# Starting a decoder trunk sooner: half a first weight unit, x through a second DMA queue, the first norm summed on VectorE, and a third unit inside that norm

## The reference

```python
hn = rmsnorm(x, norm_mix_pre[0])                 # x * rsqrt(mean(x*x) + 1e-6) * gain
proj = einsum('bsd,de->bse', u, w_in)            # u = hn
z, xBC, dt = split(proj, ...)
xBC = silu(causal_dwconv(xBC, conv_w, conv_b))   # width 4
dt = softplus(dt + dt_bias)                      # 32 heads
A = -exp(A_log)
# ssd_chunked: cumulative sums of dt*A along each chunk of 128 tokens, their exponentials, ...
```

## Time and profile before

| | |
|---|---|
| time, median of 3 runs | 1522.05 us (1521.98 to 1523.62) |
| profiled execution | 1520.41 us, of which the span is 1518.4 us |
| TensorE busy | 1460.5 us, 96% of the span |
| VectorE busy | 1021.9 us, 67% |
| ScalarE busy | 613.2 us, 40% |
| GpSimd busy | 192.4 us, 13% |
| DMA | 142.10 MB, 94 GB/s mean |

### The profile page before, as it was taken

How to read it: one execution, slowest core, us unless ns; L and a number is a source line. 1 busy time by engine, 2 the same in 40 slices (tenths; PEclk the granted TensorE clock), 3 DMA queues, 4 the chain that set the end, 5 groups by cost and what they waited for, 6 DMA issues and landing times.

```text
span 1518.4 us, 20441 instructions
## 1 busy us (share of the span) xinstructions
PE 1460.5 (96%) x6774; PEld 1162.1 (77%) x6774; DVE 1021.9 (67%) x1428; ACT 613.2 (40%) x953; POOL 192.4 (13%) x123
## 2 busy tenths in 40 slices
PE   6999999999998999999999999999789999999996
PEld 5778888888786788888888767776568888888885
DVE  6888898889427787778422667778357877776223
ACT  5654555557324323322322436565443332233221
POOL 3011100111113000000011332222121000000111
PEclk9999999999999999999999999999889999999998
DMA  4433323332221222223322121111121322223221
GB/s 150 156 125 124 138 98 137 124 138 70 84 90 63 98 97 86 94 97 105 103 95 86 54 70 56 69 55 55 42 97 56 97 97 97 95 87 112 95 95 55
DMA packets 36277, 142.10 MB, mean 94 GB/s; under 512 B 4048, under 2 KB 4176, under 8 KB 34192
## 3 DMA queue, kind: packets, MB, share of 16 engines
q1 hardware_dynamic: 36240, 141.62, 27.1%
HBM read 139.38 MB, written 2.23 MB: 93 GB/s over the span
## 4 chain that ended last, share of the span: by engine, by line
PE 75%; issue 10%; DVE 7%; POOL 3%; ACT 3%; DMA 1%; DVEq 0%; SPq 0%; POOLq 0%; ACTq 0%
PE bank L395 17%; PE bank L396 16%; PE bank L397 16%; PE b_x L395 6%; PE b_x L397 6%; PE b_x L396 6%; POOL w_lo L350 3%; DVE w_lo L358 1%; DVE cv_s L812 1%; PE b_y L828 1%; ACT w_hi L344 1%; PE b_y L395 1%; PE b_y L396 1%; PE b_y L397 1%; PE b_x L840 1%
## 5 line engine op out<-in xcount | busy, mean ns | idle before, releaser
L358 DVE TENSOR_TENSOR w_lo<-raw,w_hi 128x1024 fp32r<-128x1024 f32 (+1 forms) x190 | 254.4, 1339 | 290.4 <-ACT w_hi L344 290.2
L344 ACT ACTIVATE w_hi<-raw 128x1024 fp32r<-128x1024 f32 (+1 forms) x211 | 233.5, 1107 | 467.1 <-PE bank L397 332.3
L395 PE MATMUL bank<-hn_hi,w_hi 128*128 128x512 f32 x872 | 352.8, 405 | 15.0 <-DVE hn_lo L615 10.8
L396 PE MATMUL bank<-hn_lo,w_hi 128*128 128x512 f32 x872 | 346.8, 398 | 0.0
L397 PE MATMUL bank<-hn_hi,w_lo 128*128 128x512 f32 x872 | 346.7, 398 | 0.0
L395 PEld LDWEIGHTS bank<-hn_hi,w_hi 128*128 128x128 f32 x872 | 165.2, 189 | 58.3 <-issue 12.7
L397 PEld LDWEIGHTS bank<-hn_hi,w_lo 128*128 128x128 f32 x872 | 165.2, 189 | 40.0
L396 PEld LDWEIGHTS bank<-hn_lo,w_hi 128*128 128x128 f32 x872 | 165.4, 190 | 37.8
L395 PE MATMUL b_x<-hn_hi,w_hi 128*128 128x512 f32 x362 | 143.4, 396 | 0.0
L397 PE MATMUL b_x<-hn_hi,w_lo 128*128 128x512 f32 x362 | 143.2, 395 | 0.0
L396 PE MATMUL b_x<-hn_lo,w_hi 128*128 128x512 f32 x362 | 143.1, 395 | 0.0
(11 more groups left out here) (248 smaller groups left out, 2120.1 us busy)
## 6 DMA issues: line engine op xcount, KB each, us to landing
raw<-w_up SPq DMA_DIRECT2D x88, 512.0 KB, 3.2
raw<-w_mix SPq DMA_DIRECT2D x49, 512.0 KB, 3.3
raw<-w_dn SPq DMA_DIRECT2D x32, 704.0 KB, 4.0
raw<-w_qkv SPq DMA_DIRECT2D x24, 512.0 KB, 3.3
acs_bc<-scratch SPq DMA_DIRECT2D x8, 1024.0 KB, 5.3
ecs_bc<-scratch SPq DMA_DIRECT2D x8, 1024.0 KB, 4.7
raw<-w_sout SPq DMA_DIRECT2D x16, 512.0 KB, 3.3
raw<-w_aout SPq DMA_DIRECT2D x8, 512.0 KB, 3.4
```

The lines of the kernel that those rows point to most:

```text
L344: nc.scalar.activation(halves_of(ph, rep, first and j < 2)[0], raw[:, slot, 0:ph.width], ACT.Copy).then_inc(hi_made, 1)
L358: nc.vector.tensor_tensor(lo, raw[:, slot_of(ph, rep), 0:ph.width], hi.bitcast(F32), ALU.subtract).then_inc(lo_made, 1)
L395: nc.tensor.matmul(acc[:], wh, hi, start=first, stop=False)
L396: nc.tensor.matmul(acc[:], wh, lo, start=False, stop=False)
```

## The change

1. Unit 0 comes and is split in two halves of 512 columns. SyncE issues half, half, x chunk 2, unit 1, x chunks 3 to 7, and only then the parameters behind the first 64 columns.
2. ScalarE's queue issues x chunk 0, the 64 columns with the gains, and x chunk 1. ScalarE then runs a one-element Square, and no longer waits for all constants but for the first four.
3. The squares are added on VectorE, between the hn_lo of the chunks, and `boundary_pool` is gone from this place. Their first sum is one add of two squares instead of a copy and an add.
4. Unit 0 has its own accumulator (in b_y), so that unit 2 can start in bank 0 without waiting for it. TensorE runs chunks 0 to 2 of unit 0 alone, then those of unit 1, then both; the statistics come behind both units; unit 2 follows at once and has the spreading of the norm ahead of its chunk 2.
5. The small TensorE steps of group 0 are placed inside units: the turn of d_v ahead of chunk 6 of unit 2, the turn back of dt_tok ahead of chunk 5 of unit 4, the turn of d_acs ahead of chunk 5 of unit 5, the last-row matmul ahead of chunk 5 of unit 6.

VectorE's own order in group 0 (d_v, convolutions, dt_dve, acs_dve) is as before.

```diff
@@ trunk
+        dt_acc = b_y[:, 0, :]
@@ wait_bank
+            if ph is MIX and isinstance(j, int) and j == 2:
+                return
@@ in_unit
             for c in range(KC):
+                if mid is not None and c in mid:
+                    mid[c]()
                 last = product(acc, slot_of(ph, rep), c, ...)
@@ new: start_pe (in place of boundary_pe(pe, 0, MIX))
+            pe.wait_ge(half_lo, 1)
+            for c in range(3):
+                pe.wait_ge(hnlo_ready, c + 1)
+                chunk(0, c)
+            pe.wait_ge(lo_made, 2)
+            for c in range(3):
+                chunk(1, c)
+            for c in range(3, KC - 2):
+                pe.wait_ge(hnlo_ready, c + 1)
+                for j in range(2):
+                    chunk(j, c)
+            for j in range(2):
+                for c in (KC - 2, KC - 1):
+                    pe.wait_ge(hnlo_ready, c + 1)
+                    last = chunk(j, c)
+                last.then_inc(unit_done, 1)
+            sum_stat(pe, "pre0")
@@ new: start_act
+            act.wait_ge(consts, 4)
+            nc.scalar.activation(spare[:], eps[:], ACT.Square)
+            act.wait_ge(half_in, 16)
+            nc.scalar.activation(w_hi[:, 0, 0:HALF], raw[:, 0, 0:HALF], ACT.Copy).then_inc(half_hi, 1)
+            act.wait_ge(gain_in, 16)
+            hi(0)
+            act.wait_ge(raw_in[0], 16)
+            nc.scalar.activation(w_hi[:, 0, HALF:2 * HALF], raw[:, 0, HALF:2 * HALF], ACT.Copy).then_inc(hi_made, 1)
+            hi(1)
+            sq_of(0)
+            hi(2)
+            split_hi(act, MIX, 1, 1)
+            sq_of(1)
+            for m in range(3, KC):
+                hi(m)
+                sq_of(m - 1)
+            sq_of(KC - 1)
+            split_hi(act, MIX, 2, 2)
+            norm_root(act, norm_no["pre0"])
...
@@ new: start_dve
...
+            lo(0)
...
+            split_lo_dve(dve, MIX, 1)
+            add(1)
+            for m in range(3, KC):
+                lo(m)
+                add(m - 1)
+            split_lo_dve(dve, MIX, 2)
+            norm_diag(dve, norm_no["pre0"])
...
@@ new: mix_first_pe (in place of mix_pe(pe, 0, first=True))
+            in_unit(pe, MIX, 2, 2, {2: lambda: norm_bcast(pe, norm_no["pre0"]), 6: dt_turn})
+            in_unit(pe, MIX, 3, 3)
+            in_unit(pe, MIX, 4, 4, {5: dt_return})
+            in_unit(pe, MIX, 5, 5, {5: acs_turn})
+            in_unit(pe, MIX, 6, 6, {5: totals})
+            turn_pe(pe, 0, True)
@@ block.sync
-            load_unit(sp, MIX, 0, 0)
-            sp.dma_start(par[:], params).then_inc(par_in, 16)
+            sp.dma_start(raw[:, 0, 0:HALF], w_mix[0, :, 0:HALF]).then_inc(half_in, 16)
+            sp.dma_start(raw[:, 0, HALF:2 * HALF], w_mix[0, :, HALF:2 * HALF]).then_inc(raw_in[0], 16)
+            sp.dma_start(x[:, 2, :], x_in[:, 2, :]).then_inc(x_in_s[2], 16)
             load_unit(sp, MIX, 1, 1)
-            for m in range(KC):
+            for m in range(3, KC):
                 sp.dma_start(x[:, m, :], x_in[:, m, :]).then_inc(x_in_s[m], 16)
+            sp.dma_start(par[:, GAIN_COLS:NPAR], params[:, GAIN_COLS:NPAR]).then_inc(par_in, 16)
@@ block.scalar
+            act.dma_start(x[:, 0, :], x_in[:, 0, :]).then_inc(x_in_s[0], 16)
+            act.dma_start(par[:, 0:GAIN_COLS], params[:, 0:GAIN_COLS]).then_inc(gain_in, 16)
+            act.dma_start(x[:, 1, :], x_in[:, 1, :]).then_inc(x_in_s[1], 16)
+            start_act(act)
```

More of the change, by code:

```diff
@@ L518, in wait_x_scaled, with start_pe, chunk @@
             wait_x(eng, b, KC - 1)
+        GAIN_COLS, HALF = 8 * KC, KC * P // 2
+        def start_pe(pe):
+            def chunk(j, c):
+                return product(acc_of(MIX, j) if j else dt_acc, slot_of(MIX, j), c, hn_hi[:, c, :], hn_lo[:, c, :],
+                               c == 0, c == KC - 1)
+            pe.wait_ge(half_lo, 1)
[15 more added lines that the diff above has]
+            sum_stat(pe, "pre0")
@@ new lines, in start_dve, with lo, add @@
+        def start_dve(dve):
+            def lo(m):
+                dve.wait_ge(hnhi_ready, m + 1)
+                nc.vector.scalar_tensor_tensor(hn_lo[:, m, :], x[:, m, :], gain(0, 0, m),
+                                               hn_hi[:, m, :].bitcast(F32), ALU.mult, ALU.subtract
+                                               ).then_inc(hnlo_ready, 1)
+            def add(m):
+                dve.wait_ge(sq_ready, m + 1)
+                if m == 1:
+                    nc.vector.tensor_tensor(ssq[:], sq[:, 0, :], sq[:, 1, :], ALU.add).then_inc(sq_added, 2)
+                else:
+                    dve.wait_ge(sq_added, m)
+                    nc.vector.tensor_tensor(ssq[:], ssq[:], sq[:, m % 2, :], ALU.add).then_inc(sq_added, 1)
+            dve.wait_ge(half_hi, 1)
+            nc.vector.tensor_tensor(w_lo[:, 0, 0:HALF], raw[:, 0, 0:HALF], w_hi[:, 0, 0:HALF].bitcast(F32),
+                                    ALU.subtract).then_inc(half_lo, 1)
+            dve.wait_ge(gain_in, 16)
+            lo(0)
+            dve.wait_ge(hi_made, 1)
+            nc.vector.tensor_tensor(w_lo[:, 0, HALF:2 * HALF], raw[:, 0, HALF:2 * HALF],
+                                    w_hi[:, 0, HALF:2 * HALF].bitcast(F32), ALU.subtract).then_inc(lo_made, 1)
+            lo(1)
+            lo(2)
+            split_lo_dve(dve, MIX, 1)
[5 more added lines that the diff above has]
+            norm_diag(dve, norm_no["pre0"])
+            dve.wait_ge(rpre_copied, 1)
@@ L866, in turn_pe, with mix_first_pe, dt_turn @@
             last.then_inc(trb_ready, 1)
-        def mix_pe(pe, g, first=False):
-            if first:
+        def mix_first_pe(pe):
+            def dt_turn():
                 pe.wait_ge(dtv_ready, 1)
@@ L876, in mix_pe, with dt_return @@
                 last.then_inc(dtv_back, 1)
[L877 to L882, removed]
+            def dt_return():
                 pe.wait_ge(dt_ready, 1)
@@ L887, in mix_pe, with acs_turn @@
                 last.then_inc(dt_back, 1)
[L888 to L891, removed]
+            def acs_turn():
                 pe.wait_ge(acs_ready, 1)
@@ L897, in mix_pe, with totals @@
                 last.then_inc(dtr_ready, 1)
-            in_unit(pe, MIX, 5 + 6 * g, 5)
-            if first:
+            def totals():
                 pe.wait_ge(tok_ready, 1)
@@ L1693, in _ @@
             ch(nc.vector.tensor_copy(ones_r[:], ones[:]))
[L1694 to L1696 removed]
+            start_dve(dve)
             dve.wait_ge(unit_done, 1)
[L1698 removed]
+            dve.wait_ge(par_in, 16)
+            nc.vector.tensor_tensor(d_v[:], dt_acc[0:HS, :], r_pre[0:HS, :], ALU.mult).then_inc(evac["in"], 1)
             dve.wait_ge(evac["in"], 1)
@@ L1734, in _ @@
             pe.wait_ge(consts, N_CONST)
-            boundary_pe(pe, 0, MIX)
-            mix_pe(pe, 0, first=True)
+            start_pe(pe)
+            mix_first_pe(pe)
             with pe.Fori(1, NG) as g:
```

40 lines of the change are left out of this document (23 added, 17 removed).

## The result

| | before | changed |
|---|---|---|
| median of 5 runs | 1522.05 us (1521.87 to 1523.62) | 1530.92 us (1528.08 to 1531.97) |
| ratio, 95% interval | | 1.005 (1.0036 to 1.0065) |
| profiled execution | 1520.41 us, span 1518.4 us | 1531.97 us, span 1530.2 us |

Slower by 7.6 us by the ratio, 5.5 to 9.9 by its interval; the forecast was 5.8 us slower (1527.8). The experiments ran later, in three groups, each with the kernel before beside it; its medians there were 1523.1 to 1523.7, so each experiment is compared by its ratio.

The account below looks back on a forecast made before the run. The prediction took VectorE's chain from d_v on to bound the kernel before about 60 us, with TensorE having slack before 50 us. Terms: -1.6 + 4.0 + 3.4 = +5.8 us, forecast 1527.8 us on the median, range 1521.5 to 1530.5.

Parts of the forecast that it names:

- The mechanism: Group 0: turns inside units 4 and 5, slow after TensorE pauses of about 6 and 2.9 us, make VectorE wait.
- The wait before d_e: VectorE waits for dt_tok's turn behind 15 matmuls of unit 4, ten slow: +4.0 us, bounds 2.05 and 4.95.
- The wait before nacs: VectorE waits for d_acs's turn behind 15 matmuls of unit 5, eight slow: +3.4 us, bounds 1.9 and 4.8.
- The front: Kernel start: first matmul at about 6.4 us, statistics at 21.4, so d_v 1.6 us earlier; bounds 4.2 and 0.
- The rule I weighed in the sum: DMA at the start: queues share 16 engines, a second issuer saves only issue time; otherwise unit 1 lands at 7.3.
- Nothing behind nacs has slack: From nacs on, order on both engines is as today, with no slack for a delay to vanish in.
- The last-row matmul: Ahead of chunk 5 of unit 6: its VectorE reader is held anyway by w_hi of unit 7; nothing (0 to +1).
- Upper clock kept: Rival: TensorE keeps the upper level through both pauses before units 4 and 5; +2.4 us, 1524.4; chance 0.25.
- Weights late: Rival: unit 1's weights land 1 us later than taken, matmuls behind slow, front gains nothing; +7.4, 1529.4; chance 0.13.
- Not slower: Rival: at d_e and nacs VectorE doesn't wait for the turns, only the front counts; 1520.4 to 1517.8; chance 0.12.

Follow-up runs that it names:

- Experiment 4: Kernel before, with only the turn back of dt_tok and the turn of d_acs moved inside units 4 and 5: 1528.12 us, ratio 1.0037.
- experiment 5: Changed kernel plus 22 unread matmuls of 512 columns in TensorE's pause before unit 4: 1527.42 us, ratio 1.0025 to the kernel before.
- experiment 1: Changed kernel with both turns and the last-row matmul put back between the units: 1523.07 us, ratio 1.0005 to the kernel before.
- 2: Changed kernel with only the turn back of dt_tok put back between units 3 and 4: 1526.13 us, ratio 1.0015 to the kernel before.
- 3: Changed kernel with only the turn of d_acs put back between units 4 and 5: 1526.52 us, ratio 1.0021 to the kernel before.
- experiment 8: Experiment 1 with w_lo of units 4 to 7 made earlier, unit 6's load earlier, units 5 and 6 in own accumulators: 1533.08 us, ratio 1.0065.
- experiment 6: Experiment 1 with x chunk 0, the gains and x chunk 1 issued by SyncE in one queue: 1523.13 us, ratio 0.9996 to the kernel before.
- 7: Experiment 1 with the squares summed on GpSimd again: 1522.73 us, ratio 0.9994 to the kernel before.
- experiment 10: Experiment 6 with 12 unread matmuls ahead of the turn back of dt_tok and 7 behind it: 1522.71 us, ratio 0.9994.
- experiment 11: Experiment 6 with units 4 and 5 in b_x, w_lo of units 4 and 5 earlier, turns behind units 4 and 5: 1522.52 us, ratio 0.9991.

## Why the prediction was right, and what it mis-sized

**The mechanism was right.** Both waits are where it put them, with the releasers it named; the pauses are 5.75 and 3.07 us (forecast about 6 and 2.9); both have slow starts behind them. The measured time, 1530.92, is 3.1 us above the forecast, and 0.4 us above the range's upper end of 1530.5: the way to it was right, three of its terms were mis-sized, all to the same side.

**The wait before d_e: +4.67, forecast +4.0.** Twelve slow starts instead of the ten I took (2 x 0.194 = 0.39), and two distances are longer than 0.427 and 0.233: the first behind the pause, 0.59 (0.16 more), and the one at the step to the upper level, 0.33 (0.10 more). That is 0.65 of the 0.67. The upper bound, 4.95, held. Experiments 4 and 5 show the 2.1 without the clock.

**The wait before nacs: +3.62, forecast +3.4.** Experiment 4 has 3.52 and experiment 5 3.27 for the same wait. The forecast laid eight slow starts right behind the pause; there were seven, from the third start on, and the steps down and up took the rest.

**The front: -0.79 in the profiled execution, forecast -1.6.** The first matmul came at 7.72, not 6.4, since I took the half unit as landing at 4.23 and let the gains ride along for nothing; it landed at about 4.9, the gains held ScalarE until 5.99, and x chunk 1 until 8.21. Unit 1 landed at 8.4, close to the 8.7 of the sum, but ScalarE came to split it only at 9.97, behind the late chunks, so its w_lo was made at 12.26 and not at 11.15. TensorE never waited for it: it reached unit 1 at 12.50, right behind its nine matmuls. Against these 1.35 us stands that only three starts from there on were slow, not six (0.6 us); the statistics started at 22.27, forecast 21.4. The rule I weighed in the sum, that a second queue brings no bandwidth of its own, held for unit 1 as far as its landing shows (8.4, not 7.3), though 2.24 MB had been moved by 8.5 us and not the 1.92 I counted with; what I missed is that the second queue takes from the first transfer. Over six profiles with this front (27.20, 27.47, 26.65, 26.34, 26.30, 26.47: the changed kernel, 1, 2, 3, 5, 8) d_v is at 26.74 in the mean, and at 27.99 and 28.18 in the two with the old one: -1.3. So the term was right within 0.3 us in the mean, and that is partly luck, since two of its steps were wrong against each other; the profiled execution had a late one.

**What the front is worth.** I carried it at full value to the end. Experiments 1, 6 and 7 give 1.0005, 0.9996 and 0.9994 with intervals that all hold 1. If nothing of it reaches the end, the sum is 4.67 + 3.62 = 8.3 instead of 7.5. The traces show where it is lost in 1 and 7: 1.4 to 1.5 us behind nacs, with 12 and 13 slow starts of unit 4, and only 0.3 to 0.4 us in 6 and 10, with seven and none. In time this can't be told: the intervals of all four overlap.

**"Nothing behind nacs has slack."** Held for a delay: 7.5 us at nacs, 7.5 at 83 and 102 us, and in experiments 2, 4 and 5 the table has both marks within 0.2 us. It doesn't hold for a gain: nacs sets the time only as long as TensorE isn't later, and in 11 only 0.96 of 2.88 us are left at the mark behind. The last-row matmul, put at nothing, made wdec wait 1.24 us; in the same trace the offset stays 7.5 us after it, so it cost nothing there.

**The size.** The terms up to nacs are off by +0.8 (front), +0.67 and +0.22: +1.7. By the ratio, 7.6 us, the gap to the forecast of 5.8 is 1.8, and they fill it, with the profiled execution's late front; with the mean front they come to 1.2. By the medians it is 3.1, and 1.4 of that stay open: 0.9 joins slowly up to 385 us, half of it by the longer round of the loop, and the rest is within the spread of medians (the kernel before itself was at 1523.1 to 1523.7 later, 1.1 to 1.6 above the median I counted from).

**The rivals.** "Upper clock kept" is false as written (both pauses cost slow starts), and experiment 5 shows its world for unit 4. "Weights late" didn't happen as meant: unit 1 landed at 8.4, not at 9.7. "Not slower" is refuted by experiments 1 to 4.

## What to carry to other kernels

Before a small step is moved into a unit of work, ask what starts that unit. Here the unit was waiting for the very engine that was next to need the small step, so 15 matmuls went into that engine's chain; in the gap ahead of the unit the step had been free. An engine that finishes early and then stands isn't just not faster: its next work ran at half the clock for 12 matmuls, which cost 2.5 us exactly where the critical engine waited. And when a dependency is taken away, look up the next one of the same instruction (weights, then accumulator, then load) before counting the gain, as experiment 8 teaches. The same holds for a shorter critical chain: in experiment 11 nacs came 2.88 us earlier and 0.96 of that was left, because TensorE had become the later one.

## What was unexpected of the hardware

- A pause of 5.75 us before unit 4 is followed by 12 slow starts at once, one of 3.07 us before unit 5 by seven that begin with the third start (from the fourth start on eight in experiment 4, and six at once in experiment 5). In experiment 1 two pauses, 3.44 and 1.71 us with a turn of 0.6 us between them, are followed by 13, and in experiment 6 two of 3.43 and 1.28 us by seven. In group 0 none follows pauses of 0.39 to 0.93 us. So the length of the pause doesn't scale the price.
- Nor does it alone decide whether there is one. The pause of 1.00 us at 109.56 us of experiment 1 is followed by seven slow starts (granted clock 0.83 from 110 to 120 us), the same pause at 108.25 of experiment 6 by none; and so it was with the 0.47 us of the kernel before and the changed one near 1070 us.
- In the first 14 us starts are 0.43 apart while the granted clock is given as 1.00:

```profile
8.00:14.00 6.00, 5.57 (x13) 3.69 (x13) 4.60 (x7) 5.03 (x8) 0.00 (x0) 1.00 1.01 368
```

  So for the start of a kernel the distances between starts have to be read, and not that column. How long this phase lasts differs between executions, from six slow starts (experiment 11) to 20 (experiment 10).
- Gains of 32 KB took 4.8 us to land beside larger transfers of two queues, and 3.1 us in one; the first 256 KB took 4.2 and 2.6 us.
